# A feed-forward block whose gate and up products are made from seven block products instead of eight

## The reference

```python
D_FF_2 = -(-8 * D_MODEL // (3 * 256)) * 256            # 2816 = 22 hidden tiles of 128

h2 = rms_norm_2(x, norm2_gain[l]) * (1.0 + sc2) + sh2
x = x + gt2 * ((jax.nn.silu(h2 @ ffn_w_gate[l]) * (h2 @ ffn_w_up[l])) @ ffn_w_down[l])
```

## Time and profile before

| | |
|---|---|
| median of 3 runs | 2516.86 us (2516.19 to 2516.89) |
| span of the profiled execution, first to last instruction | 2515.7 us |
| PE busy in the span | 2497.5 us, 99% |
| DVE, ACT, GpSimd busy | 1385.6, 941.3, 60.5 us |
| granted TensorE clock, mean | 0.999 |
| HBM traffic | 103 GB/s over the span |

### The profile page before, as it was taken

The page is one execution under the profiler, slowest core; times in us unless marked ns, Lnnn a source line. Parts: engine busy times, 40 slices in busy tenths (PEclk is TensorE's granted clock), DMA queues, the critical chain, the costliest instruction groups (busy, mean ns, idle before and its releaser), DMA issues.

```text
span 2515.7 us, 29885 instructions
## 1 busy us (share of the span) xinstructions
PE 2497.5 (99%) x11809; PEld 2024.1 (80%) x11809; DVE 1385.6 (55%) x1902; ACT 941.3 (37%) x1359; POOL 60.5 (2%) x77
## 2 busy tenths in 40 slices
PE   9999999999999999999999999999999999999999
PEld 7788888888888877888888888887877768888887
DVE  5556356544556745555664444567554676733433
ACT  5432233422334444123342233445543573422222
POOL 6000000000000000000001000000000001000000
PEclk9999999999999999999999999999999999999999
DMA  4122222444433222232234333222321212222222
GB/s 165 67 84 85 100 101 93 159 151 151 142 138 122 88 84 68 86 103 97 95 140 138 117 125 125 101 89 98 117 84 67 68 35 68 101 100 101 96 88 100
DMA packets 38627, 260.02 MB, mean 103 GB/s; under 512 B 4416, under 2 KB 4672, under 8 KB 8048
## 3 DMA queue, kind: packets, MB, share of 16 engines
q1 hardware_dynamic: 32976, 226.92, 26.5%
q10 hardware_dynamic: 5296, 30.20, 3.4%
q0 software_dynamic: 240, 1.28, 0.2%
HBM read 256.29 MB, written 2.10 MB: 103 GB/s over the span
## 4 chain that ended last, share of the span: by engine, by line
PE 95%; DVE 3%; ACT 1%; issue 1%; DMA 0%; SPq 0%; DVEq 0%; ACTq 0%
PE ps L2043 65%; PE ps L2070 9%; PE ps L2278 6%; PE ps L2096 5%; PE ps L2220 2%; PE ps L2262 2%; PE ps L2242 1%; DVE w_lo L1166 1%; PE ps L2504 1%; PE ps L2520 1%; PE ps L2196 0%; DMA h<-x_t 0%; PE ps L2560 0%; PE ps L2366 0%; ACT w_hi L771 0%
## 5 line engine op out<-in xcount | busy, mean ns | idle before, releaser
L1166 DVE TENSOR_TENSOR w_lo<-raw,w_hi 128x2048 fp32r<-128x2048 f32 x208 | 477.4, 2295 | 325.1 <-ACT w_hi L598 275.2
L2043 PE MATMUL ps<-a_hi,w_hi 128*128 128x512 f32 x1408 | 550.4, 391 | 0.3 <-DVE w_lo L1166 0.3
L2043 PE MATMUL ps<-a_hi,w_lo 128*128 128x512 f32 x1408 | 547.9, 389 | 0.0
L2043 PE MATMUL ps<-a_lo,w_hi 128*128 128x512 f32 x1408 | 547.8, 389 | 0.0
L598 ACT ACTIVATE w_hi<-raw 128x2048 fp32r<-128x2048 f32 x198 | 376.4, 1901 | 404.3 <-PE ps L2043 338.3
L2043 PEld LDWEIGHTS ps<-a_hi,w_hi 128*128 128x128 f32 x1408 | 264.3, 188 | 56.9 <-issue 1.1
L2043 PEld LDWEIGHTS ps<-a_hi,w_lo 128*128 128x128 f32 x1408 | 264.3, 188 | 55.3
L2043 PEld LDWEIGHTS ps<-a_lo,w_hi 128*128 128x128 f32 x1408 | 264.3, 188 | 55.1 <-issue 1.0
L2043 PE MATMUL ps<-f_hi,w_hi 128*128 128x512 f32 x708 | 275.4, 389 | 0.0
L2043 PE MATMUL ps<-f_lo,w_hi 128*128 128x512 f32 x708 | 275.4, 389 | 0.0
L2043 PE MATMUL ps<-f_hi,w_lo 128*128 128x512 f32 x708 | 275.4, 389 | 0.0
(11 more groups left out here) (387 smaller groups left out, 3539.9 us busy)
## 6 DMA issues: line engine op xcount, KB each, us to landing
raw<-weights SPq DMA_DIRECT2D x209, 1024.0 KB, 4.8
ada_w<-ada ACTq DMA_DIRECT2D x24, 1024.0 KB, 4.9
merged<-cmp_w SPq DMA_DIRECT2D x2, 1024.0 KB, 5.9
out<-h SPq DMA_DIRECT2D x8, 256.0 KB, 2.0
h<-x_t SPq DMA_DIRECT2D x3, 512.0 KB, 8.0
raw<-weights SPq DMA_DIRECT2D x4, 256.0 KB, 5.6
kt<-c_row ACTq DMA_DIRECT2D x2, 512.0 KB, 3.5
pads<-p_t ACTq DMA_DIRECT2D x2, 512.0 KB, 4.0
```

What stands on the lines that cost most here:

```text
L1166: dve.tensor_tensor(w_lo[n % 2][:, w], raw[n % 2][:, w], w_hi[n % 2][:, w].bitcast(F32), ALU.subtract)\
L2043: ins = pe.matmul(dst, a[i], b[j], start=done == 0, stop=done == total - 1)
```

## The change

The twenty inner hidden tiles are made in ten groups of two. For a group the weights are a 2x2 matrix of blocks, gate or up (row) by first or second half of the 1024 input features (column), each block 512x256 features, that is 128x1024 in SBUF. The input is a 2x2 matrix too: half of the features by half of the tokens, `x11`, `x12`, `x21`, `x22`. Its product takes eight block products; the changed kernel takes seven (`A11`, `S1`, `S2`, `A12`, `S3`, `A22`, `S4`), some of them with sums of weight blocks and with differences of input blocks. A block product is 2 output tiles x 4 k-tiles x 3 = 24 matmuls with 128x256 moving elements.

- The input sums (`mix_12`, `mix_3`, `mix_4`) are made once: ACT writes an unrounded copy of the normed input (`keys`, `wide_too` in `norm_high`), GpSimd makes four sums of 128x1024 from it, ACT rounds them, DVE makes their rests.
- The weight sums are made for each group: S1, S2 and S4 by a GpSimd addition of 128x1024 in SBUF, S3 by a DMA of GpSimd that accumulates in SBUF onto the block A11.
- The ring of split weights now has four slots of 128x1024; ACT and DVE split the weights of a job three jobs ahead (`AHEAD`).
- The chain of each group runs in one bank: `A11`, then `S2`, `S3` and `A22` are added on top, and ACT copies the bank in between (`first_copy`, `second_copy`, `third_copy`).
- `ffn_down` is made as eight jobs a chunk, half a unit each; its matmuls are the same in number and shape.
- `dynamic_dma_scratch_size=8192` is given, so that there is room for the sums.

```diff
+GROUPS = (3, 4, 3)
+AHEAD = 3
+def job_order():
+    order, group, last = [("A11", 0), ("S1", 0)], 0, sum(GROUPS) - 1
+    for c, groups in enumerate(GROUPS):
+        for j in range(group, group + groups):
+            order += [("S2", j), ("A12", j), ("S3", j)]
+            order += [("S1", j + 1), ("A22", j), ("A11", j + 1)] if j < last else [("A22", j)]
+            order += [("S4", j)]
+        order += [("down", 8 * c + i) for i in range(8)]
+        group += groups
...
SP
+            sp.wait_ge(sem("norm_r"), 2 * DEPTH)
+            load_sum(0)
+            load_sum(1)
+            load_sum(2)
...
GpSimd
+            def second_sum(j):
+                pool.wait_ge(*part_low("S1", j))
+                pool.wait_ge(*block_loaded("A11", j)[1])
+                add_to_sum("S2", j, block_a11[j % 2])
+            def third_sum(j):
+                pool.wait_ge(*part_low("A11", j))
+                pool.wait_ge(*block_loaded("S2", j)[1])
+                x, (added, _) = block_loaded("S3", j)
+                pool.dma_start(x, weight_block(1, 0, j), accum_op=ALU.add).then_inc(added, 16)
...
+            first_sum(0)
+            x11, x12, x21, x22 = x_wide
+            pool.wait_ge(sem("wide_made"), KT)
+            pool.tensor_tensor(x22, x22, x12, ALU.subtract).then_inc(sem("mix_made"), 1)
+            pool.tensor_tensor(x12, x11, x12, ALU.subtract).then_inc(sem("mix_made"), 1)
+            pool.wait_ge(sem("mix_made"), 2)
+            pool.tensor_tensor(x11, x11, x22, ALU.add).then_inc(sem("mix_made"), 1)
+            pool.wait_ge(sem("mix_made"), 3)
+            pool.tensor_tensor(x21, x11, x21, ALU.subtract).then_inc(sem("mix_made"), 1)
+            second_sum(0)
+            third_sum(0)
+            first_sum(1)
+            for j in range(NG):
+                fourth_sum(j)
+                if j + 1 < NG:
+                    second_sum(j + 1)
+                    third_sum(j + 1)
+                if j + 2 < NG:
+                    first_sum(j + 2)
...
ACT
-            norm_high(24, {4: (n + 2, ST["ffn_next"][1])})
+            norm_high(24, {}, wide_too=True)
...
+            high("A11", 0)
+            high("S1", 0)
             act.wait_ge(sem("first_gate"), 1)
             act.activation(T[1][:, :], T[0][:, :], ACT.Tanh, scale=0.5).then_inc(sem("ff_tanh"), 1)
+            mix_high(0, mix_12[:, 0, :], x_wide[1], 2)
             x_high(f_hi[:, 0, :], T[2][:, :])
+            act.wait_ge(*tile_done(g_next))
+            act.activation(T[0][:, :], bank(g_next)[:, :], ACT.Tanh, scale=0.5).then_inc(sem("ff_tanh"), 1)
+            mix_high(1, mix_12[:, 2, :], x_wide[0], 3, scale=-1.0)
+            high("S2", 0)
+            mix_high(2, mix_3[:, 0, :], x_wide[3], 3)
+            act.wait_ge(sem("mix_low"), 2)
+            mix_high(3, mix_4[:, 0, :], x_wide[2], 4)
+            x_high(f_hi[:, 1, :], T[2][:, :])
+            ahead("A11", 0)
+            first_copy(0)
+            ahead("S1", 0)
...
PE
+            def product(kind, j, x, to, opens, closes):
+                q = JOB[kind, j]
+                pe.wait_ge(*part_low(kind, j))
+                w = ring(w_hi, q % 4), ring(w_lo, q % 4)
+                for m in range(2):
+                    for k in range(4):
+                        cols = slice(256 * k + P * m, 256 * k + P * m + P)
+                        for a, b in ((0, 0), (0, 1), (1, 0)):
+                            ins = pe.matmul(to[:, 256 * m:256 * m + 256], w[a][:, cols], x[b][:, k, :],
...
+            chain_opened(0)
+            side_opened(0)
+            for c, js in stages_of_groups():
+                for j in js:
+                    pe.wait_ge(sem("copied"), 3 * j + 1)
+                    if j == 0:
+                        pe.wait_ge(sem("mix_low"), 2)
+                    product("S2", j, m_mix, chain_bank(j), False, False)
```

More of the change, by code:

```diff
@@ L459, in copies @@
             return x.unsqueeze(1).to_broadcast([P, n, x.shape[-1]])
+        ORDER = job_order()
+        JOB = {x: q for q, x in enumerate(ORDER)}
+        NG = sum(GROUPS)
+        g_first, g_next = ST["ffn_first"][1], ST["ffn_next"][1]
+        blocks = [yq[:, 2 * i:2 * i + 2, :] for i in range(4)]
+        blocks += [raw[(ST["ffn_first"][0] + i // 2) % 2][:, 1024 * (i % 2):1024 * (i % 2) + 1024] for i in range(4)]
+        blocks = [x.rearrange("p a n -> p (a n)") if len(x.shape) == 3 else x for x in blocks]
@@ new lines, in chain_bank, with side_bank, down_bank, hidden_tiles @@
+        def chain_bank(j):
+            return ps[j % 2]
+        def side_bank(j):
+            return ps[4 - j % 2]
+        def down_bank(u, j):
+            return ps[((5, 6), (7, 2))[u % 2][j]]
+        def hidden_tiles(x, j, half):
+            c = sum(j >= sum(GROUPS[:i + 1]) for i in range(2))
+            k = 2 * (j - sum(GROUPS[:c])) + (0 if c else 2)
+            return x[:, k:k + 2, 256 * half:256 * half + 256]
+        def two_tiles(x):
+            return x.rearrange("p (a n) -> p a n", a=2)
@@ L461, in program, with four_tiles, stages_of_groups @@
+        def four_tiles(x):
+            return x.rearrange("p (a n) -> p a n", a=4)
+        def stages_of_groups():
+            group = 0
+            for c, groups in enumerate(GROUPS):
+                yield c, range(group, group + groups)
+                group += groups
         block = ctx.enter_context(nc.Block())
@@ L1124, in _, with mix_high @@
+            def mix_high(i, dst, src, made, scale=1.0):
+                act.wait_ge(sem("mix_made"), made)
+                act.activation(four_tiles(dst), src, ACT.Copy, scale=scale).then_inc(sem("mix_high"), 1)
+            high("A11", 0)
+            high("S1", 0)
             act.wait_ge(sem("first_gate"), 1)
             act.activation(T[1][:, :], T[0][:, :], ACT.Tanh, scale=0.5).then_inc(sem("ff_tanh"), 1)
+            mix_high(0, mix_12[:, 0, :], x_wide[1], 2)
             x_high(f_hi[:, 0, :], T[2][:, :])
[L1127 to L1144, removed]
@@ L2000, in _ @@
             x_low(f_lo[:, 0, :], T[2][:, :], f_hi[:, 0, :])
[L2001 to L2009, removed]
-                    else:
[L2011 to L2025, removed]
@@ L2628, in _ @@
             first_hidden = [c.next("x_made"), evacuated(ST["ffn_next"][1] + 1)]
[L2629 to L2633, removed]
+            x11, x12, x21, x22 = [[x[:, 4 * (i // 2):4 * (i // 2) + 4, 256 * (i % 2):256 * (i % 2) + 256] for x in A]
+                                  for i in range(4)]
@@ L2705, in lay_out @@
         n = P * tiles
[L2706 to L2708 removed]
+        units.append(feature_units(f("ffn_w_down_2")[0][at:at + n], tiles, 256))
         at += n
```

359 lines of the change are left out of this document (352 added, 7 removed).

## The result

The changed kernel takes 2521.1 us (median of 14 runs, 2520.2 to 2526.2); the kernel before took 2516.9 us beside it (14 runs, 2515.7 to 2519.2). The ratio is 1.0018, with a 95% interval of 1.0011 to 1.0025: 4.2 us slower. The interval is 2.8 to 6.3 us, so the bound of 0.2% (5.0 us) that the prediction sets lies inside it. The forecast was 2521.2 us and 4.3 above before. One run of before beside the last experiment took 2763.0 us at a granted clock of 0.851, a slower state of the chip, and is left out of all comparisons.

A forecast was written before the change was run, and what follows sets the result against it. PE was taken to bound the kernel, busy 99% of the span, so each matmul less saves time and each PE wait loses it. 2516.9 - 16.0 (matmuls) + 18.6 (opening) + 1.7 (clock) = 2521.2 us, range 2510 to 2531.

The forecast's parts named there:

- Matmuls, -16.0: Inner hidden tiles: 960 matmuls of 128x512 (217.6 us) replaced by 1680 of 128x256 (201.6 us), a gain of 16.0 us.
- The opening, +18.6: Group 0, A11 to A12: PE waits while GpSimd's additions and DVE's SBUF operations exclude each other, 18.6 us lost.
- the list: Step-by-step schedule of group 0's opening on the old clock; A12 ends at 2205.0 against 2186.4 if nothing were late.
- offset additions: First hidden tile on DVE: one SBUF input, taken as not waiting for GpSimd; in a two-port mode 0.75 us more.
- Clock, +1.7: Opening: one dip of PE's granted clock behind its waits, not hidden, 1.7 us; 0 and 4 are the ends.
- a sign for the opening: New profile, 2175 to 2210: PE's waits for DVE's and ACT's operations would sum to 15 to 20 us.
- The groups, 0: Groups of 20.2 us: DVE and GpSimd need 19.5 to 20.8, slack covers the lag, no loss taken.
- the tightest wait: In each group, the copy for S3: 2.0 us of work in 5.8 available; 0 lost.
- The sign that PE idles under 0.5 us in each group: New profile: the groups' forecast of no loss is right if PE idles under 0.5 us in each.
- Product boundaries: 70 boundaries with semaphore waits: nothing taken; rival says 0.05 to 0.1 us each, 3.5 to 7 us, chance 0.09.
- slower by over 0.2%: Outcome for the whole kernel: slower than before by more than 0.2% (5.0 us), chance 0.49.
- within 0.2%: Outcome for the whole kernel: difference from before under 0.2% (5.0 us), about what measurement can't tell from none; chance 0.36.

The follow-up runs named there:

- the last experiment: Changed kernel with hidden tiles 2 and 3 made as plain units and GpSimd's sums spread over both, complete: 2509.7 us, ratio 0.9973 to before.
- e5: Kernel before with the 960 matmuls of its inner hidden tiles issued as 1920 of 128x256, complete: 2528.7 us, 12.4 above before.
- e3: Changed kernel with GpSimd's input sums and weight sums S1, S2, S4 all cut to 8 columns: 2508.3 us, 12.5 below the changed kernel.
- e1: Changed kernel with GpSimd's four input sums cut to 8 columns each: 2515.4 us, 5.5 below the changed kernel.
- e2: Changed kernel with GpSimd's thirty weight-block additions (S1, S2, S4) cut to 8 columns: 2513.9 us, 7.0 below the changed kernel.
- e4: Changed kernel with the four input sums made by DVE instead of GpSimd, complete: 2519.1 us, 1.7 below the changed kernel.
- e6: Changed kernel with hidden tiles 2 and 3 made as plain units, then nine groups of seven products, complete: 2515.9 us, 0.4 under before.

## Why the prediction was right

- **Matmuls, -16.0.** Right: 0.1200 us in all stretches of the groups, and e5 gives 12.4 us for the narrow shape alone where the two distances give 12.8.
- **The opening, +18.6.** Measured 19.35. Laid on the clock of before (0.73 us added, after 2100) the starts of A11, S1, S2 and A12 were 79.8, 89.3, 96.6 and 102.9, where the list had 79.8, 88.8, 96.6 and 102.1. Its split is another matter. The list gives about 10 us to GpSimd's additions (9.5, as 18.6 less 9.1) and 9.1 to DVE's own queue, and calls 9.1 the lower bound. Without the additions 6.6 to 6.9 us are left (e3, and 19.35 less 12.5), and 2.5 of these are clock, so the queue costs about 4; the additions cost 12.5 (e1 5.5, e2 7.0). The two errors nearly cancel. Which steps of the list hold them was not followed up; the offset additions are one.
- **The offset additions.** I had left them out of the waiting ones. The trace shows 3.73 us for two instead of 0.87, and 0.87 again in e4, where no sum of GpSimd stood there. The prediction names this case and prices it at 0.75 us; the two were stretched by 2.9. By the rule of the Trainium skill (SBUF — State Buffer, Who interferes with whom) an operation with one SBUF input waits only where it runs in a two-port mode, which a `tensor_scalar` can; the trace agrees that such a one can wait, and no run here shows the mode itself.
- **Clock, +1.7.** The mechanism was there, the price was not: PE fell to the 1.2 GHz level behind its waits, and all of it lay in time that PE would have waited: the chain to A12 runs through DVE, which waits for PE nowhere in it. ACT waits for PE once, 1.60 us before its copy at 2200.30, which A12 doesn't need. Windows of the changed kernel (columns as in those of e3):

```profile
2180.00:2184.00 4.00, 3.70 (x19) 3.50 (x17) 3.94 (x3) 1.58 (x2) 2.88 (x2) 0.57 0.00 0
...
2188.00:2192.00 4.00, 3.46 (x16) 3.46 (x17) 4.00 (x4) 1.26 (x2) 3.44 (x3) 0.50 0.00 0
...
2204.00:2208.00 4.00, 4.00 (x36) 4.00 (x35) 3.56 (x4) 1.06 (x1) 3.32 (x1) 1.00 0.96 326
```

  The first is A11, the second S1, the last is behind A12: 20 products from A12 on took 57.83 us, 0.2 more than at full clock. The prediction had set a sign for the opening, PE's waits adding to 15 to 20 us, and this sign failed: they add to 11.1 us from A11 to A12, 12.5 with the one for the last `a_lo`. Between the starts of A11 and A12 the slow matmuls fill 5.8 us more, time that the list had as idle. Where the opening is shorter, the clock comes into the open (2.5 us each in e3 and e4).
- **The groups, 0.** 1.0 us more than before, of which 0.7 is one wait for the copy behind S3 (`third_copy`) in the last group. The prediction had named this copy as the tightest wait, for what it needs before it; here it began when S3 had ended and its own 0.6 us showed, since the last group has no S1 of a next one between S3 and A22. The sign that PE idles under 0.5 us in each group failed there by 0.2. GpSimd's additions cost the groups nothing (e2). Product boundaries cost nothing that can be told from the 0.1200.
- What I had named wrongly: PE's waits for ACT. There were none in the opening of the changed kernel; DVE ended each.
- That gain and loss came out within 0.1 us of the forecast is luck in part, with errors of both signs: 0.75 too little in the opening, 1.0 too little in the groups, 1.7 too much for the clock, and inside the opening the split above. The chances put slower by over 0.2% first, at 0.49, and within 0.2%, where the median fell, at 0.36.

## What to carry to other kernels

Price a fast algorithm by the measured distance of its matmuls: half the columns took 53% of the time (0.1200 to 0.2267), and of an eighth less work (27 us) 16 us were left. Moving additions to an idle GpSimd costs DVE what is left of each addition that one of its SBUF operations meets (1.4 to 2.2 us each here), so they belong where DVE has slack for PE; here the weight sums of the steady groups were free, and eight additions at the start, with DVE on the critical path, cost 12.5 us. A start-up that goes to another place meets the queues there: look on each engine for what stands ahead of the next operation that PE wants; e6 moved the sums and lost 8 us to one split. A loss of clock can be hidden by the waits around it and show when they go: e3 and e4 each had 2.5 us of it that the changed kernel didn't.

## What had not been expected of the hardware

- A DVE operation on one SBUF input (`T<-T,offset`, 128x512) waits for a GpSimd addition like one on two: 3.73 us for two beside additions, 0.87 without; 4.04 in e6.
- GpSimd's addition of 128x1024 was 2.39 us alone, 2.82 us where a DVE operation of 512 columns took its turn first and 3.2 to 3.3 where one of 1024 did; in the opening the two engines took turns one for one.
- An accumulating DMA of 512 KB from GpSimd's queue landed in 5.5 us in the median, the plain weight loads of the same size in 3.7 to 5.1; its issue held GpSimd for 0.9 us, and PE never waited for it.
